# Sixteen expert units of the way in split beside pass A's front and read back; three slots beside each ranking unit

## The chip, the cores and the metric

The kernel runs on one core of a Trainium2 chip. The metric is the device time of one execution in microseconds. The kernel before was timed three times: 3121.53, 3127.26 and 3132.98 us, so its median is 3127.26 us. The profile is of a separate execution.

Engine names are those of the profile: PE is TensorE (PEld its weight loads), DVE is VectorE, ACT is ScalarE, POOL is GpSimd and SP is SyncE, which here only issues transfers.

## The reference, cut to what matters

The reference is one encoder layer on 1024 tokens of width 1024:

```python
h   = LN(x) * (1 + scale1) + shift1            # scale, shift, gate from silu(c) @ w_cond
u, v, gB, gC, z, ga, gb = split(h @ w_in)      # "the front"
yA  = gelu(u) * (W_s @ LN(gelu(v)) + b)        # spatial gating inside 128-position blocks
yB  = gB * conv3_causal(gC * z)
m   = sigmoid(ga) * (yA @ P_A) + sigmoid(gb) * (yB @ P_B)
x   = LN(alpha * x + gate1 * (m @ W_o))
h2  = LN(x) * (1 + scale2) + shift2
# experts: 8 heads, product keys, top 16 of 16384 experts per head and token
q       = h2 @ w_q
s1, s2  = q_half0 @ keys0.T, q_half1 @ keys1.T
top 16 of s1[i] + s2[j]  ->  idx, gate = softmax(top)
act     = gelu(sum_d expert_u[idx] * h2)       # "the way in"
ffn     = sum_k gate * act * expert_v[idx]     # "the way out"
x   = LN(alpha * x + gate2 * ffn)
```

All of it is float32 in the reference.

## The kernel before

**Two passes over the tokens.** Pass A is token blocks 0 to 2 (384 tokens), pass B blocks 3 to 7 (640 tokens). Both go through the front: units of 1 MB of weights, named V (4), C (12), U (4), M (16), O (4), and Q (8, one for each head's query). For pass B the experts are computed densely: 64 units E of `expert_u` (the way in, 256 experts a unit), then 64 units W of `expert_v` (the way out) in 32 groups of two. For pass A the chosen rows are gathered: 384 slots (3 blocks x 8 heads x 16), and for each slot one gathered row of `expert_u` (a dot product with h2 on DVE, `u_row`, L1050) and one of `expert_v` (a weighted sum on DVE, `v_row`, L1059). POOL issues these gathers, each 128 rows of 4 KB. The table `SECTION` says how many slots are worked off beside which unit of pass B.

**Split weights.** Every product is done with float16 halves: a 1 MB float32 unit is multiplied by 256 and split into a high and a low half, and each output takes three matmuls (high x high, high x low, low x high; L1626 to L1628). The split of unit n takes a load into one of two `stage` buffers (SP, L555), the high half by ACT (`make_hi`, L712, `w<-stage`) and the low half by DVE (`make_lo`, L954), both into slot n mod 4 of `w`. The split of unit n+4 is done after unit n has been evacuated. In pass A the 48 front units are split and both halves are also stored to `hl_dram` (1 MB, SP, L535); pass B reads them back from there straight into `w` (L564), without ACT and DVE.

**The order.** `_order` writes the units out in one list, `UNITS`, and every engine goes through this list: PE in `feature_unit` and `token_tile`, ACT and DVE in a loop over the list, SP in `load`. `CONVERTED` says which units are split, `V_OF` numbers them. SP issues in order. `load` of split number v first stores the halves of number v-2 to `hl_dram` and waits for `lo_done` of number v-2, which is what makes its stage buffer free. Beside the loads of pass A's front SP also issues `cond_pair`, 1 MB of `w_cond` after every second unit, 16 times; DVE takes their dot products (L1032).

**The ranking.** Beside the units E0 to E35 DVE also ranks pass B's scores (`rank`, in pieces, 8 heads). Then DVE makes the softmax (`gates`, L1359 to L1363, at E37), PE transposes indices and gates (L1794, after E38), and DVE copies them (`idx_t`, L1388, at E39). Beside E40 to E59 one-hot products spread the gates ("spreading units"). Before the change a unit E0 to E39 has 2 or 3 slots in turn, E40 to E59 have 2, E60 to E63 have 4, and the 30 first groups of the way out share the rest, 5 or 6 each. The rows land in rings of buffers: 6 buffers ("rank") for E0 to E36, 4 ("own") for E37 to E39.

Of the kernel before, what the change touches and what calls it, by code (L numbers as in the profile page):

```python
# [10 lines left out]
F16 = mybir.dt.float16  # L11
# [40 lines left out]


def _order():

    order = [("A", kind, u) for kind in "VCUMO" for u in range(COUNT[kind])]
    order += [("B", "V", u) for u in range(4)]
# [20 lines left out]
N_OF = {u: n for n, u in enumerate(UNITS)}  # L78
CONVERTED = [x == "A" or kind in "EW" for x, kind, _ in UNITS]
V_OF = [sum(CONVERTED[:n]) for n in range(len(UNITS))]  # L80
N_FRONT_CONV = sum(COUNT.values())


def _tiles():

    at, first, number = 0, [], []
    for x, kind, u in UNITS:
        if kind == "W":
            k = 0
        elif kind in "VO":  # L90
            k = NBLK[x]
        else:
            k = 2 if x == "A" else 4
        first.append(at)
        number.append(k)
        at += k
    return first, number
# [32 lines left out]
def _stores():  # L130

    seen, at = [0] * NW, {}
    for n in range(len(UNITS)):
        if CONVERTED[n] and V_OF[n] < N_FRONT_CONV:
            seen[n % NW] += 1
            at[n] = seen[n % NW]
    return at


STORES = _stores()  # L140
CONV_N = [n for n in range(len(UNITS)) if CONVERTED[n]]


# [47 lines left out]
def _sections():  # L191
# [6 lines left out]
    for e in range(2 * NGRP):  # L198
        k["B", "E", e] = 2 + e % 2 if e < E_SPREAD else 2 if e < E_SPREAD + N_SPREAD else 4
    groups = NGRP - 2  # L200
# [77 lines left out]
def trunk_layer(nc, x, c_row, w_cond, b_col, w_front, ln_g, ln_b, w_spat, b_spat, conv_w,  # L278
                ln1_g, ln1_b, keys_t, u_units, v_units, u_rows, v_rows, ln2_g, ln2_b, out):
    with ExitStack() as ctx:  # L280
# [150 lines left out]

        hl_dram = nc.dram_tensor("hl_dram", [48, P, 2, 2048], F16).ap()
        mod_dram = nc.dram_tensor("mod_dram", [48, P], F32).ap()
# [97 lines left out]
        def _(sp):  # L531
            def store_hl(n):
                sp.wait_ge(lo_done, V_OF[n] + 1)
                f = FRONT[UNITS[n][1]] + UNITS[n][2]
                sp.dma_start(hl_dram[f], w[:, n % NW]).then_inc(hl_stored[n % NW], 16)  # L535

            stored = [0]

            def store_to(v):

                while stored[0] <= min(v, N_FRONT_CONV - 1):
                    store_hl(CONV_N[stored[0]])
                    stored[0] += 1

            def load(n):
                x, kind, u = UNITS[n]
                if CONVERTED[n]:
                    v = V_OF[n]
                    store_to(v - 2)
                    if v >= 2:  # L550
                        sp.wait_ge(lo_done, v - 1)
                    if (x, kind, u) in (("B", "E", 0), ("B", "E", 1)):
                        sp.wait_ge(row_used, FRONT_ROWS)
                    src = u_units[u] if kind == "E" else v_units[u] if kind == "W" else w_front[FRONT[kind] + u]
                    sp.dma_start(stage[:, v % 2, :], src).then_inc(stage_in[v % 2], 16)  # L555
                    return
                f = FRONT[kind] + u
                m = N_OF["A", kind, u]
                if CONVERTED[n - NW]:
# [24 lines left out]
            sp.dma_start(ws_t, w_spat).then_inc(ws_in, 16)  # L584
            n_a = len([u for u in UNITS if u[0] == "A" and u[1] != "Q"])
            for n in range(4, n_a):
                load(n)
                if 4 <= n < 36 and n % 2 == 0:
                    cond_pair(8 + (n - 4) // 2)
                if n == 5:  # L590
# [119 lines left out]
        def _(act):  # L710
# [89 lines left out]
            for n, (x, kind, u) in enumerate(UNITS):  # L800
                if kind == "W":
                    break
                t = T_OF[n]
                if (x, kind, u) in H_AT:
# [133 lines left out]
        def _(dve):  # L938
# [497 lines left out]
            for n, unit in enumerate(UNITS):  # L1436
                x, kind, u = unit
                if kind == "W":
                    break
                if x == "A" and kind != "Q" and n % 2 == 0 and n >= 2 and pair < n_pairs:  # L1440
                    cond_dots(pair)
# [174 lines left out]
        def _(pe):  # L1616
# [105 lines left out]
            for n, (x, kind, u) in enumerate(UNITS):  # L1722
                if kind == "W":
                    break
                hl = (h_hi[x], h_lo[x])
                if (x, kind, u) == ("A", "M", 13):
# [155 lines left out]
```

## Time and profile before

| | |
|---|---|
| median of three runs | 3127.26 us |
| profiled execution, its own time | 3120.44 us |
| its span, first to last instruction | 3118.6 us |
| PE busy | 2916.0 us (94%) |
| DVE busy | 2555.4 us (82%) |
| ACT busy | 840.0 us (27%) |
| POOL busy | 1026.4 us (33%) |
| bytes moved by DMA | 917.52 MB, mean 294 GB/s |

Busy shares are averages over stages with different limits, so they are read stage by stage. Pass A's front is about 40 to 410 us, pass B's front to about 1110 us, E0 to E39 to about 1770 us, the spreading units and E60 to E63 to about 2240 us, and the way out from there to the end. A matmul's duration in a row is longer than its distance to the next one, since matmuls overlap in the pipeline: how fast PE goes is read from how many matmuls it starts in a stretch. PEclk 1.00 is 2.4 GHz, 0.50 is 1.2 GHz. Times of DMA are from issue to landing.

### The profile page before, as it was taken

The page shows a single profiled execution, that of the slowest core. Times are in us where ns is not written, and L with a number is a line of the kernel's source. Part 1 is how long each engine was busy: PE and PEld are TensorE (multiplying, and loading weights), DVE is VectorE, ACT ScalarE, POOL GpSimd, SP SyncE. Part 2 cuts the span into 40 slices and gives each one's busy share as a digit, 9 for nine tenths or more (in the row PEclk, how much of TensorE's full clock was granted, in tenths as well). Part 3 has the DMA queues.
Part 4 walks back from the last instruction along what each step waited for, and adds up shares of the span by engine and source line. Part 5 has one row for each costly group of instructions (what it writes and reads, how often), then busy time and mean ns, then how long its engine had stood idle before and what let it go on. Part 6 is the DMA issues. An engine that isn't in the chain of part 4 may idle for free.

```text
span 3118.6 us, 47106 instructions
## 1 busy us (share of the span) xinstructions
PE 2916.0 (94%) x19088; PEld 1914.8 (61%) x19088; DVE 2555.4 (82%) x4744; ACT 840.0 (27%) x1242; POOL 1026.4 (33%) x778
## 2 busy tenths in 40 slices
PE   4899999997998799999999699999789999999997
PEld 3565686765776566677777488888534444444443
DVE  5865556998777678999999788888589999999878
ACT  3333432211111332222223133333222222222220
POOL 0000000004665024444454422222455555555410
PEclk8999999998999899999999899999899999999999
DMA  8888653435999257788888788888999999999972
GB/s 344 306 312 315 238 193 122 136 129 193 344 395 351 88 201 286 298 302 312 307 323 304 291 288 283 289 291 292 354 371 396 398 395 394 398 390 408 349 265 116
DMA packets 266233, 917.52 MB, mean 294 GB/s; under 512 B 20464, under 2 KB 102432, under 8 KB 222752
## 3 DMA queue, kind: packets, MB, share of 16 engines
q1 hardware_dynamic: 63968, 427.91, 35.8%
q0 software_dynamic: 110592, 402.70, 34.6%
q10 hardware_dynamic: 91456, 83.89, 8.3%
q8 instruction: 151, 2.47, 0.3%
q14 instruction: 66, 0.54, 0.0%
HBM read 771.79 MB, written 142.63 MB: 293 GB/s over the span
## 4 chain that ended last, share of the span: by engine, by line
PE 39%; DVE 7%; DMA 3%; issue 2%; POOL 1%; ACT 0%; DVEq 0%; POOLq 0%
PE psU L1626 7%; PE psU L1627 7%; PE psU L1628 7%; PE psX L1627 5%; PE psX L1628 5%; PE psX L1626 5%; PE psX L1778 5%; DMA rows<-in_v_rows,idx_sp 3%; DVE acc_sp L1059 1%; DVE w L954 1%; POOL rows L705 1%; DMA Z<-in_v_rows,idx_sp 0%; DVE rows L1050 0%; DVE Z L1278 0%; DVE Z L1268 0%
## 5 line engine op out<-in xcount | busy, mean ns | idle before, releaser
L1626 PE MATMUL psU<-hB,w 128*128 128x320 f16 (+1 forms) x3072 | 923.7, 301 | 13.3 <-DVE hB L1025 6.9
L1628 PE MATMUL psU<-hB,w 128*128 128x320 f16 (+1 forms) x3072 | 920.5, 300 | 0.0
L1627 PE MATMUL psU<-hB,w 128*128 128x320 f16 (+1 forms) x3072 | 920.4, 300 | 0.0
L712 ACT ACTIVATE w<-stage 128x2048 f16<-128x2048 f32 x176 | 335.9, 1910 | 540.7 <-PE psX L1628 368.6
L954 DVE SCALAR_TENSOR_TENSOR w<-stage,w 128x2048 f16<-128x2048 f32 x176 | 402.4, 2287 | 93.0 <-ACT w L712 92.9
L705 POOL DMA_INDIRECT rows<-in_u_rows,idx_sp x217 | 286.4, 1320 | 525.1 <-DVE rows L1050 364.7
L1626 PEld LDWEIGHTS psU<-hB,w 128*128 128x128 f16 x3072 | 304.5, 99 | 128.0 <-DVE hB L1025 7.6
L1628 PEld LDWEIGHTS psU<-hB,w 128*128 128x128 f16 x3072 | 301.3, 98 | 119.6 <-issue 0.8
L1627 PEld LDWEIGHTS psU<-hB,w 128*128 128x128 f16 x3072 | 304.6, 99 | 112.8 <-issue 0.8
L705 POOL DMA_INDIRECT rows<-in_v_rows,idx_sp x219 | 288.2, 1316 | 245.7 <-DVE rows L1050 142.2
L1626 PE MATMUL psU<-w,Z 128*128 128x512 f16 (+1 forms) x768 | 268.8, 350 | 52.7 <-DVE Z L1428 30.3
L1059 DVE SCALAR_TENSOR_TENSOR acc_sp<-rows,weight_sp,acc_sp 128x1024 f32<-128x1024 f32 x219 | 275.8, 1288 | 47.2 <-DMA rows<-in_v_rows,idx_sp 34.5
L1626 PE MATMUL psX<-w,Z 128*128 128x512 f16 x768 | 291.1, 379 | 3.1 <-DVE Z L1549 3.1
L1627 PE MATMUL psX<-w,Z 128*128 128x512 f16 x768 | 291.1, 379 | 0.0
L1628 PE MATMUL psX<-w,Z 128*128 128x512 f16 x768 | 291.1, 379 | 0.0
L1050 DVE SCALAR_TENSOR_TENSOR rows<-rows,h_sp 128x1024 f32<-128x1024 f32 x217 | 259.3, 1222 | 26.6 <-DMA rows<-in_u_rows,idx_sp 25.3
L1627 PE MATMUL psU<-w,Z 128*128 128x512 f16 (+1 forms) x768 | 268.4, 349 | 0.0
L1628 PE MATMUL psU<-w,Z 128*128 128x512 f16 (+1 forms) x768 | 268.1, 349 | 0.0
L712 ACT ACTIVATE Z<-psU 128x320 f32<-128x320 f32 (+3 forms) x224 | 99.9, 453 | 518.5 <-PE psU L1628 496.0
L712 ACT ACTIVATE R<-psU 128x320 f32<-128x320 f32 (+1 forms) x296 | 123.9, 427 | 393.7 <-PE psU L1628 393.4
L1627 PE MATMUL psU<-Z,w 128*128 128x384 f16 (+1 forms) x640 | 206.1, 322 | 0.0
L1628 PE MATMUL psU<-Z,w 128*128 128x384 f16 (+1 forms) x640 | 206.0, 322 | 0.0
(252 smaller groups left out, 4504.4 us busy)
## 6 DMA issues: line engine op xcount, KB each, us to landing
stage<-in_u_units SPq DMA_DIRECT2D x64, 1024.0 KB, 8.9
stage<-in_v_units SPq DMA_DIRECT2D x64, 1024.0 KB, 7.8
stage<-in_w_front SPq DMA_DIRECT2D x48, 1024.0 KB, 7.6
hl_dram<-w SPq DMA_DIRECT2D x48, 1024.0 KB, 5.6
w<-hl_dram SPq DMA_DIRECT2D x48, 1024.0 KB, 7.8
a_dram<-R ACTq DMA_DIRECT2D x64, 640.0 KB, 8.3
g_dram<-Z ACTq DMA_DIRECT2D x20, 2048.0 KB, 15.3
Z<-a_dram SPq DMA_DIRECT2D x32, 1280.0 KB, 11.7
```

What stands on the lines that cost most here:

```text
L705: pool.indirect_dma_start(row_at[r], None, u_rows if table == "u" else v_rows, bass.IndirectOffsetOnAxis(ap=idx_sp[:, slot:slot + 1], axis ...
L712: return nc.scalar.activation(dst, src, func, scale=scale)
L954: V.scalar_tensor_tensor(w[:, n % NW, 1, :], stage[:, v % 2, :], WS, w[:, n % NW, 0, :], ALU.mult, ALU.subtract).then_inc(lo_done, 1)
L1050: V.scalar_tensor_tensor(row_at[r], row_at[r], 1.0, h2_sp[:, slot % SB, :], ALU.mult, ALU.mult, accum_out=dots[:, c % 8, j:j + 1]).then_in ...
L1059: V.scalar_tensor_tensor(dst, row_at[r], weight_sp[:, slot:slot + 1], dst, ALU.mult, ALU.add).then_inc(row_used, 1)
L1626: mm(ps, lhs[0](k), rhs[0](k), start=start and s == 0, stop=False)
L1627: mm(ps, lhs[0](k), rhs[1](k), start=False, stop=False)
L1628: last = mm(ps, lhs[1](k), rhs[0](k), start=False, stop=stop and s == n - 1)
L1778: ins = mm(ps[:, t * P:(t + 1) * P], oh_keys[:, q % 4, 0, :, t], oh_gate[:, q % 4, c, :, t], start=(c == 0), stop=(c == 1))
```

## The change

1. `EARLY` names the expert units E1, E3, ..., E31 (16 units). Each gets a new entry ("P", "P", u) in the unit list of pass A's front: after the 9th unit of pass A, the 11th, and so on to the 39th (after C4, C6, ..., O2). A P entry is loaded into `stage`, split by ACT and DVE into its slot of `w` and stored to `hl_dram`, but PE has no work for it.
2. In pass B these 16 units are no longer split; they are read from `hl_dram` into `w`, as the front's units are. `hl_dram` grows from 48 to 64 units. `home` says where the halves of a unit lie.
3. `SECTION`: units E0 to E35 have 3 slots each, E36 to E39 have 2. The way out's groups get 4 or 5 instead of 5 or 6. The sum over E0 to E63 goes from 156 to 172 slots of 384.
4. `cond_pair` and the dots of w_cond keep their places by counting pass A's own units, without P.

```diff
+EARLY = list(range(1, 33, 2))
 def _order():
-    order = [("A", kind, u) for kind in "VCUMO" for u in range(COUNT[kind])]
+    order = []
+    for kind in "VCUMO":
+        for u in range(COUNT[kind]):
+            order.append(("A", kind, u))
+            at = sum(x == "A" for x, _, _ in order)
+            if at > 8 and at % 2 == 1 and (at - 9) // 2 < len(EARLY):
+                order.append(("P", "P", EARLY[(at - 9) // 2]))
...
-CONVERTED = [x == "A" or kind in "EW" for x, kind, _ in UNITS]
+CONVERTED = [x in "AP" or kind == "W" or kind == "E" and u not in EARLY for x, kind, u in UNITS]
...
+def home(n):
+    x, kind, u = UNITS[n]
+    if kind in "PE":
+        return sum(COUNT.values()) + EARLY.index(u), N_OF["P", "P", u]
+    return FRONT[kind] + u, N_OF["A", kind, u]
...
-        k["B", "E", e] = 2 + e % 2 if e < E_SPREAD else 2 if e < E_SPREAD + N_SPREAD else 4
+        k["B", "E", e] = 3 if e < E_SPREAD - 4 else 2 if e < E_SPREAD + N_SPREAD else 4
...
-        hl_dram = nc.dram_tensor("hl_dram", [48, P, 2, 2048], F16).ap()
+        hl_dram = nc.dram_tensor("hl_dram", [N_STORED, P, 2, 2048], F16).ap()
...
                 if kind == "W":
                     break
+                if x == "P":
+                    make_hi(n + NW)
+                    continue
...
+                if x == "P":
+                    make_lo(n + NW)
+                    continue
```

**SP, pass A's front.** In the list of the kernel before, about the tenth load of a unit, a pair of units has two loads, two stores and one load of w_cond:

```order
L535 DMA hl_dram<-w 128x4096
L555 DMA stage<-in_w_front 128x2048
L535 DMA hl_dram<-w 128x4096
L555 DMA stage<-in_w_front 128x2048
L568 DMA hB<-in_w_cond 128x2x1024
```

The same place in the changed kernel (L552 is the store, L572 the load into `stage`, L584 `cond_pair`):

```order
L552 DMA hl_dram<-w 128x4096
L572 DMA stage<-in_u_units 128x2048
L552 DMA hl_dram<-w 128x4096
L572 DMA stage<-in_w_front 128x2048
L552 DMA hl_dram<-w 128x4096
L572 DMA stage<-in_w_front 128x2048
L584 DMA hB<-in_w_cond 128x2x1024
```

One load of `u_units` and one store have come in for each pair of units; everything else stands as it did.

**DVE, the last ranking units.** Before, from the split beside E37 (the first row) to the copies of the transposed indices at E39 (L1388):

```order
L954 SCALAR_TENSOR_TENSOR w<-stage,w 128x2048
L1359 TENSOR_REDUCE Z<-Z 128x40
L1361 RECIPROCAL Z<-Z 128x40
L1363 TENSOR_TENSOR Z<-Z 128x640
L1050 SCALAR_TENSOR_TENSOR rows,dots<-rows,h_sp 128x1024 x3
L1059 SCALAR_TENSOR_TENSOR acc_sp<-rows,weight_sp,acc_sp 128x1024 x3
L1072 SCALAR_TENSOR_TENSOR weight_sp<-dots,gate_sp 128x2
L954 SCALAR_TENSOR_TENSOR w<-stage,w 128x2048
L1050 SCALAR_TENSOR_TENSOR rows,dots<-rows,h_sp 128x1024 x2
L1059 SCALAR_TENSOR_TENSOR acc_sp<-rows,weight_sp,acc_sp 128x1024 x2
L1072 SCALAR_TENSOR_TENSOR weight_sp<-dots,gate_sp 128x3
L1388 CAST Z<-psX 128x384
```

And in the changed kernel (L975 is the split, L1071 and L1080 the rows, L1409 the copy):

```order
L975 SCALAR_TENSOR_TENSOR w<-stage,w 128x2048
L1380 TENSOR_REDUCE Z<-Z 128x40
L1382 RECIPROCAL Z<-Z 128x40
L1384 TENSOR_TENSOR Z<-Z 128x640
L1071 SCALAR_TENSOR_TENSOR rows,dots<-rows,h_sp 128x1024 x2
L1080 SCALAR_TENSOR_TENSOR acc_sp<-rows,weight_sp,acc_sp 128x1024 x2
L1093 SCALAR_TENSOR_TENSOR weight_sp<-dots,gate_sp 128x3
L975 SCALAR_TENSOR_TENSOR w<-stage,w 128x2048
L1071 SCALAR_TENSOR_TENSOR rows,dots<-rows,h_sp 128x1024 x2
L1080 SCALAR_TENSOR_TENSOR acc_sp<-rows,weight_sp,acc_sp 128x1024 x2
L1093 SCALAR_TENSOR_TENSOR weight_sp<-dots,gate_sp 128x3
L1409 CAST Z<-psX 128x384
```

Here one slot fewer stands beside E37. Further up, beside E0 to E35, every even unit has one slot more, and 16 of the splits are gone.

## Rows read from the trace of the kernel before

**Rows 1.** Busy us by stretch: PE, PEld, DVE, ACT, POOL; then PEclk, DMA share, GB/s
```profile
100.00:340.00 240.00, 234.26 (x1434) 142.63 (x1432) 161.05 (x180) 82.86 (x90) 0.00 (x0) 0.99 0.84 317
...
1125.00:1760.00 635.00, 600.77 (x4417) 436.19 (x4416) 585.11 (x1663) 163.89 (x286) 303.07 (x224) 0.98 0.82 303
...
2280.00:3000.00 720.00, 720.00 (x3338) 326.39 (x3337) 659.57 (x705) 174.27 (x110) 384.84 (x275) 1.00 0.98 385
```

**Rows 2.** DMA issues of the page: KB each, median us to landing
```profile
stage<-in_w_front SPq DMA_DIRECT2D x48, 1024.0 KB, 7.6
hl_dram<-w SPq DMA_DIRECT2D x48, 1024.0 KB, 5.6
...
Z<-in_w_cond SPq DMA_DIRECT2D x12, 1024.0 KB, 10.3
```

**Rows 3.** ACT in order of time: evacuations that end units, 7.8 us apart
```profile
246.30 0.49 ACT L712 ACTIVATE Z<-psU 128x384 f32<-128x384 f32 x1 [3.35 <-PE psU L1628]
...
254.10 0.49 ACT L712 ACTIVATE Z<-psU 128x384 f32<-128x384 f32 x1 [3.35 <-PE psU L1628]
...
261.90 0.49 ACT L712 ACTIVATE Z<-psU 128x384 f32<-128x384 f32 x1 [3.35 <-PE psU L1628]
```

**Rows 4.** The costliest groups of the page: the two halves of a split
```profile
L712 ACT ACTIVATE w<-stage 128x2048 f16<-128x2048 f32 x176 | 335.9, 1910 | 540.7 <-PE psX L1628 368.6
L954 DVE SCALAR_TENSOR_TENSOR w<-stage,w 128x2048 f16<-128x2048 f32 x176 | 402.4, 2287 | 93.0 <-ACT w L712 92.9
```

**Rows 5.** SP in order of time: load number 9, the first that moves
```profile
112.50 0.33 SPq L535 DMA_DIRECT2D hl_dram<-w  x1
112.87 0.44 SPq L555 DMA_DIRECT2D stage<-in_w_front  x1
```

**Rows 6.** SP in order of time: the last load of pass A's front
```profile
359.48 0.33 SPq L535 DMA_DIRECT2D hl_dram<-w  x1
359.85 2.24 SPq L555 DMA_DIRECT2D stage<-in_w_front  x1
```

**Rows 7.** DVE in order of time: the last low half of pass A's front
```profile
376.60 2.28 DVE L954 SCALAR_TENSOR_TENSOR w<-stage,w 128x2048 f16<-128x2048 f32 x1
```

**Rows 8.** ACT in order of time: last evacuations of O2 and of O3
```profile
402.10 0.38 ACT L712 ACTIVATE acc_sp<-psU 128x256 f32<-128x256 f32 x1 [2.24 <-PE psU L1628]
...
409.96 0.38 ACT L712 ACTIVATE acc_sp<-psU 128x256 f32<-128x256 f32 x1 [2.24 <-PE psU L1628]
```

**Rows 9.** Short stretches of pass A's front, columns as in rows 1
```profile
120.00:140.00 20.00, 20.00 (x125) 12.05 (x124) 14.14 (x15) 8.34 (x9) 0.00 (x0) 1.00 0.99 389
...
232.00:236.00 4.00, 1.44 (x9) 0.67 (x7) 1.93 (x3) 2.29 (x2) 0.00 (x0) 1.00 0.99 303
236.00:240.00 4.00, 3.35 (x11) 1.61 (x12) 4.00 (x5) 0.00 (x0) 0.00 (x0) 0.58 1.00 417
```

**Rows 10.** Waits of PE, 1700 to 1770 us: total, times, longest
```profile
PE psX L1794 <- DVE Z L1388: 22.1, 1, 22.1
PE psX L1794 <- DVE Z L1363: 5.7, 1, 5.7
```

**Rows 11.** DVE groups, 1125 to 1760 us: busy us, mean ns, idle before
```profile
L1059 DVE SCALAR_TENSOR_TENSOR acc_sp<-rows,weight_sp,acc_sp 128x1024 f32<-128x1024 f32 x76 | 96.1, 1289 | 27.4 <-DMA rows<-in_v_rows,idx_sp 18.5 <-issue 8.5
L1050 DVE SCALAR_TENSOR_TENSOR rows<-rows,h_sp 128x1024 f32<-128x1024 f32 x80 | 95.0, 1222 | 12.4 <-DMA rows<-in_u_rows,idx_sp 11.4
L954 DVE SCALAR_TENSOR_TENSOR w<-stage,w 128x2048 f16<-128x2048 f32 x40 | 91.6, 2290 | 0.0
```

**Rows 12.** Waits of DVE, 1700 to 1770 us
```profile
DVE acc_sp L1059 <- DMA rows<-in_v_rows,idx_sp: 10.4, 5, 4.2
DVE acc_sp L1059 <- issue: 4.5, 1, 4.5
```

More of the change, by code:

```diff
@@ L78 @@
 N_OF = {u: n for n, u in enumerate(UNITS)}
-CONVERTED = [x == "A" or kind in "EW" for x, kind, _ in UNITS]
+CONVERTED = [x in "AP" or kind == "W" or kind == "E" and u not in EARLY for x, kind, u in UNITS]
 V_OF = [sum(CONVERTED[:n]) for n in range(len(UNITS))]
-N_FRONT_CONV = sum(COUNT.values())
+N_STORED = sum(COUNT.values()) + len(EARLY)
 def _tiles():
@@ L87, in _tiles @@
     for x, kind, u in UNITS:
-        if kind == "W":
+        if kind in "WP":
             k = 0
@@ L133, in _stores @@
     for n in range(len(UNITS)):
-        if CONVERTED[n] and V_OF[n] < N_FRONT_CONV:
+        if CONVERTED[n] and V_OF[n] < N_STORED:
             seen[n % NW] += 1
@@ L533, in store_hl @@
                 sp.wait_ge(lo_done, V_OF[n] + 1)
-                f = FRONT[UNITS[n][1]] + UNITS[n][2]
-                sp.dma_start(hl_dram[f], w[:, n % NW]).then_inc(hl_stored[n % NW], 16)
+                sp.dma_start(hl_dram[home(n)[0]], w[:, n % NW]).then_inc(hl_stored[n % NW], 16)
             stored = [0]
             def store_to(v):
-                while stored[0] <= min(v, N_FRONT_CONV - 1):
+                while stored[0] <= min(v, N_STORED - 1):
                     store_hl(CONV_N[stored[0]])
@@ L551, in load @@
                         sp.wait_ge(lo_done, v - 1)
-                    if (x, kind, u) in (("B", "E", 0), ("B", "E", 1)):
+                    if v in (N_STORED, N_STORED + 1):
                         sp.wait_ge(row_used, FRONT_ROWS)
-                    src = u_units[u] if kind == "E" else v_units[u] if kind == "W" else w_front[FRONT[kind] + u]
+                    src = u_units[u] if kind in "PE" else v_units[u] if kind == "W" else w_front[FRONT[kind] + u]
                     sp.dma_start(stage[:, v % 2, :], src).then_inc(stage_in[v % 2], 16)
                     return
-                f = FRONT[kind] + u
-                m = N_OF["A", kind, u]
+                f, m = home(n)
                 if CONVERTED[n - NW]:
@@ L584, in _ @@
             sp.dma_start(ws_t, w_spat).then_inc(ws_in, 16)
-            n_a = len([u for u in UNITS if u[0] == "A" and u[1] != "Q"])
+            n_a = N_OF["B", "V", 0]
+            pairs = 8
             for n in range(4, n_a):
                 load(n)
-                if 4 <= n < 36 and n % 2 == 0:
-                    cond_pair(8 + (n - 4) // 2)
+                if UNITS[n][0] == "A" and n >= 4 and pairs < 24 and sum(u[0] == "A" for u in UNITS[:n]) % 2 == 0:
+                    cond_pair(pairs)
+                    pairs += 1
                 if n == 5:
@@ L1439, in _ @@
                     break
-                if x == "A" and kind != "Q" and n % 2 == 0 and n >= 2 and pair < n_pairs:
+                if x == "P":
+                    make_lo(n + NW)
+                    continue
+                if x == "A" and kind != "Q" and n >= 2 and pair < n_pairs and sum(v[0] == "A" for v in UNITS[:n]) % 2 == 0:
                     cond_dots(pair)
@@ L1724, in _ @@
                     break
+                if x == "P":
+                    continue
                 hl = (h_hi[x], h_lo[x])
```

## The prediction

> **What bounds the kernel now.** I read the busy shares by stretch first, then the waits of PE, then each engine in order of time where PE waits. In pass A's front PE is busy 234 of 240 us while the DMA engines are busy 84% of the time at 317 GB/s [rows 1]: PE sets the pace, and the transfers are not far behind. A unit takes 7.8 us there [rows 3]. In the stage of the ranking units PE is busy 601 of 635 us, but DVE 585 of 635 [rows 1], and at its end PE stands still for 22.1 + 5.7 us until DVE has made the gates and copied the transposed indices [rows 10]. DVE is the engine that is late there, and its own waits are for gathered rows [rows 11, 12]: the length of this stage is DVE's work. On the way out PE is busy 720 of 720 us at full clock, and it starts 3338 matmuls of 512 columns in 720 us, one in 215.7 ns, against 512 / 2.4 GHz = 213.3 ns [rows 1]. DVE is at 92% and DMA at 98% there without holding PE up.
>
> **Way out: gain 0.** The change takes 16 slots from the way out, 16 x (1.289 + 1.222) = 40 us of DVE [rows 11] and 16 MB of gathers. PE is at 99% of its rate and waits for neither engine. The most that could come is 720 x (215.7 - 213.3) / 215.7 = 8 us; I take 0.
>
> **Pass A's front: transfers.** Per pair of units the kernel before moves two loads, two stores and one pair of w_cond, each 1 MB [rows 2]: 5 x 1.049 = 5.24 MB in 15.6 us, 336 GB/s. The change adds a load and a store for each pair: 7.34 MB in the same 15.6 us would be 470 GB/s. What the engines can do: 317 GB/s at a share of 0.84 is 377 GB/s at a full share [rows 1], and the best 20 us of this front show 389 [rows 9]. So 7.34 MB take 7.34 / 0.377 = 19.5 us: the transfers become the bound, by 3.9 us a pair.
>
> The DMA page of the Trainium skill ("DMA: Bandwidth & Descriptors", Specifications) puts the limit of the memory at about 358 GB/s per core. Rows 9 show 389 in 20 us, so here the trace does not agree; by the page a period would take 20.5 us, and the sum below would be 13 us larger.
>
> **Pass A's front: the stage ring.** There are two stage buffers. One of them goes round like this: issue 0.4 us, landing 7.6 us [rows 2], high half 1.91, low half 2.29 [rows 4], and about 0.2 us of semaphores: 12.4 us for a load, so 6.2 us a load with two buffers, 18.6 us for three loads. This is nearly the same as 19.5, so where w_cond is moved too the transfers decide (19.5), and where it is not (6.29 MB, 16.7 us) the ring decides (18.6).
>
> **Pass A's front: the sum.** The first P entry is load number 9, which before was issued at 112.9 us [rows 5]; pass A's last unit O3 was number 39, issued at 359.9 [rows 6], and becomes number 55. From 9 to 55 there are 46 loads: 13 periods of three with w_cond, 13 x 19.5 = 253.5 us, and 7 loads of 6.2 = 43.4. O3 is issued at 112.9 + 297 = 410 us, 50 us later. Before, its low half was ready at 376.6 + 2.3 = 378.9 [rows 7], and PE began it when O2 was through, at 402.1 [rows 8]: a lead of 23 us, which is used up first. After: 410 + 0.4 + 7.6 + 1.9 + 2.3 = 422 us against 402, +20 us. To this comes that the ring does not run ideally: ACT makes the high half only after it has evacuated a unit, and DVE makes the low half after the convolution, merge and w_cond work that stands before it in its order. With two limits so close together (18.6 and 19.5) such delays add up instead of hiding. I take 1 us for each of about 14 periods, somewhat less than one product of w_cond with c (1.2 us, like the row of the same size in rows 11): +14. **Front: +34 us.** From both sides: if nothing but bytes counts, 16 x 2.10 = 33.6 MB / 0.377 = 89 us of transfers, less the free share of 100 to 340 us, 0.16 x 240 = 38, less the lead of 23, and less what the easier last 7 loads leave (some 10): +18. If every load lands only after 10.3 us, as w_cond does [rows 2], the ring takes 15.1 / 2 = 7.6 us a load: 46 x 7.6 = 348 us, O3's load at 461, so +71. ACT and DVE themselves have room: 83 and 161 of 240 us busy [rows 1], and 1.9 and 2.3 more per pair of 15.6 us. After the front pass B's units run on PE alone, so the delay is not made good later.
>
> **Ranking units.** DVE's list up to the copies at E39 has 97 slots beside E0 to E38 before and 114 after, 17 more: 17 x 2.51 = 42.7 us. It loses 16 low halves: 16 x 2.29 = 36.6 [rows 11]. Net +6; since instructions overlap a little in the trace, +5. The 16 units read back cost the same 1 MB as before, SP issues them when PE has left the slot (unit n-4), and PE needs them three units later, some 39 us: hidden. ACT loses 16 high halves; nobody waits for them. Row waits: in this stage DVE is idle 27.4 + 12.4 us before rows in `rows` [rows 11], some 0.4 us a slot. 17 more slots, with 17 MB more on DMA engines that are busy 82% [rows 1], make +7; the units E37 and E38, whose rows share four buffers and behind which 10.4 + 4.5 us are waited [rows 12], have one slot fewer: -4. **Ranking: +8 us.** Bounds: -10, if the 15 us of rows 12 go altogether, and +25, if the row waits grow by half. The wait of PE at the gates stays and grows by this amount.
>
> **Sum.** 34 + 8 = +42 us: 3120.4 + 42 = 3162 us for an execution like the profiled one. That one is 7 us under the median of the three runs, so I put the median after at 3127.3 + 42 = **3169 us**.
>
> **Rivals.**
> 1. *The front hides it, and the ranking stage gets shorter (faster).* The lead of 23 us and the free 16% of the DMA engines swallow the 33.6 MB, and with two slots each beside E36 to E39 the row waits before the copies go (-10). Median 3117. Point of decision: 46 loads would have to pass in 247 + 23 = 270 us, 5.9 us each, so a period in 17.6 us, which is 417 GB/s. The rows of this front show that only for 4 us [rows 9]. Chance 0.07; and 0.06 that the front costs so little that the two cancel (3118 to 3137).
> 2. *The ring is slower than computed.* Landing goes to 10 us, since each load stands behind a store and a pair of w_cond in the queue: 22 us a period, +37 over the forecast: 3206. For it: loads of w_cond land in 10.3 us [rows 2]. Against it: the loads before landed in 7.6 at 84% busy engines. Chance 0.15.
> 3. *PE's clock falls.* Every period PE would starve for some 4 us. After 2.6 us without work from 232 to 236 us the granted clock of the next stretch is 0.58, close to 1.2 GHz [rows 9]. If half of the matmuls of each period run at 1.2 GHz, a pair of units takes 15.6 x 1.5 = 23.4 us, over the 19.5 of the transfers: +3.9 x 14 = 55 over the forecast, 3224. Against it: a slow stretch of 4 us costs 2 us of PE's work, and a period has 3.9 us to spare. Chance 0.06. The page "TensorE: Matmul & The Clock Gate" of the Trainium skill (HAM oscillation) tells of such a kernel, which waits for a transfer in each round and starts each round at the slow clock; rows 9 agree as to the fall, and no row of before shows it repeated.
> 4. *The ranking stage pays more than the front.* The rows come late with three slots beside each unit and six buffers: ranking +25 and front as forecast: 3186. It lies in the range; chance 0.06.
>
> **How the numbers follow.** The forecast has 0.60, with its own range of 3145 to 3195 (front +18 to +55, ranking 0 to +15). The range 3135 to 3206 leaves out rival 1, most of rival 3 and a part of rival 2, some 0.2. A change under 0.3%, about 9 us, could not be told from none for this kernel. Faster is rival 1, 0.07; same is 0.06; slower is the rest, 0.87.
>
> **What the changed profile would show.** DMA share at 0.95 or more at 370 to 390 GB/s from about 115 to 400 us; PE waiting for the low half of `w` in each period, with granted clock below 1.00 in some of them; load number 55 issued at about 410 to 425 us; the end of O3 near 440 us instead of 410. The stage from E0 to the copies of the indices 0 to 15 us longer, with PE's wait at the transposes of about 35 us. The way out as long as before, with DVE's busy share lower by 40 us. It would be wrong if PE stayed busy through the front (rival 1), if periods took 22 us or more (rival 2), or if the way out became shorter by more than 8 us.

## The result: slower by 3.4%, outside the forecast range

| | median us | runs |
|---|---|---|
| before | 3130.12 | 3121.53 to 3134.93 (4) |
| after | 3236.66 | 3229.83 to 3243.77 (4) |

The ratio is 1.0344, with an interval of 1.0311 to 1.0377. That is +106.5 us where +42 was forecast, and 3236.7 against a range that ended at 3206. The profiled execution of after took 3243.8 us with a span of 3242.0, 123.4 us above the span of before. It lies 7 us over the median of its runs and the one of before lay 10 us under its own, so 17 of the 123 belong to the two executions and not to the change.

The span divides at the last evacuation of O3 (end of pass A's front), the first store of a ranking unit (E0), the copies of the transposed indices, and the first unit of the way out:

| stage | before | after | difference | forecast |
|---|---|---|---|---|
| start to the end of O3 | 410.0 | 478.6 | +68.6 | +34 |
| to E0 | 721.7 | 742.0 | +20.3 | 0 |
| E0 to the copies of the indices | 625.5 | 664.8 | +39.3 | +8 |
| to the way out | 520.4 | 515.5 | -4.9 | 0 |
| way out | 841.0 | 841.1 | +0.1 | 0 |

The forecast had the two right places and was low at both by about the same amount.

**Pass A's front.** Busy us of PE, PEld, DVE, ACT and POOL, then granted clock, DMA share and GB/s, first in the whole front of before, then of after with four short stretches of it:

```profile
100.00:410.00 310.00, 297.52 (x1910) 191.03 (x1909) 191.77 (x225) 113.75 (x144) 0.00 (x0) 0.98 0.78 288
```

```profile
100.00:479.00 379.00, 307.74 (x1898) 194.66 (x1897) 226.70 (x237) 139.33 (x159) 0.00 (x0) 0.90 0.86 323
200.00:220.00 20.00, 5.22 (x33) 5.03 (x33) 14.42 (x15) 6.49 (x5) 0.00 (x0) 0.65 0.93 349
220.00:240.00 20.00, 20.00 (x117) 11.86 (x116) 11.82 (x13) 6.74 (x7) 0.00 (x0) 0.92 0.45 168
380.00:400.00 20.00, 6.35 (x35) 4.15 (x32) 13.23 (x15) 7.36 (x7) 0.00 (x0) 0.67 0.97 379
400.00:420.00 20.00, 12.97 (x74) 8.24 (x75) 7.79 (x9) 9.78 (x14) 0.00 (x0) 0.73 0.63 244
```

PE does the same work, idles 71.3 us instead of 12.5, and its busy time grows by 10.2 because the granted clock falls from 0.98 to 0.90. The DMA share is not the 0.95 at 370 to 390 GB/s that the forecast named but 0.86 at 323: PE and the transfers stand still in turn. From 200 to 220 us PE works 5 of 20 us while DMA runs at 0.93, and in the next 20 us PE works throughout while DMA falls to 0.45. So neither of the two is the bound on its own.

Who waits for whom, in after's front: waits of PE (total, times, longest), then of ACT and DVE.

```profile
PE psU L1650 <- DVE w L975: 21.4, 6, 5.4
PE psX L1707 <- DVE h_sp L1198: 14.8, 1, 14.8
PE psX L1755 <- DVE modc L1470: 12.6, 1, 12.6
PE psU L1650 <- issue: 10.7, 1, 10.7
PE psX L1696 <- DVE Z L1475: 8.1, 1, 8.1
```

```profile
ACT w L730 <- DMA stage<-in_w_front: 102.1, 30, 5.2
ACT w L730 <- DMA stage<-in_u_units: 66.2, 12, 7.2
```

```profile
DVE w L975 <- ACT w L730: 109.8, 39, 6.2
DVE acc_sp L1240 <- DMA Z<-in_ln_b: 15.6, 1, 15.6
```

Only 21 us of PE's waits are for a low half, as forecast. Most of the others are for DVE work that has nothing to do with a split (h_sp of the mixing, modc, Z): it stands on DVE behind a split that waits for ACT, which waits for a load. The 10.7 us to which the profile gives no releaser ("issue") are of the same kind: PE's matmul at 263.81 us reads the `acc_sp` that DVE writes from 262.75 to 263.71 (L1214), behind the split of 258.96. In its whole front (100 to 410 us) ACT of the kernel before waited for stage loads 8 times, 17.1 us in all; here it is 42 times and 168.3 us. One such place, ACT, DVE and PE at the mixing in order of time (the bracket holds the idle time ahead and its releaser):

```profile
205.13 1.91 ACT L730 ACTIVATE w<-stage 128x2048 f16<-128x2048 f32 x1 [2.96 <-DMA stage<-in_w_front]
...
212.00 1.91 ACT L730 ACTIVATE w<-stage 128x2048 f16<-128x2048 f32 x1 [4.20 <-DMA stage<-in_w_front]
```

```profile
213.94 2.29 DVE L975 SCALAR_TENSOR_TENSOR w<-stage,w 128x2048 f16<-128x2048 f32 x1 [2.12 <-ACT w L730]
216.15 2.48 DVE L1198 TENSOR_TENSOR h_sp<-psX,Z 128x512 f32<-128x512 f32 x4
```

```profile
216.88 1.44 PE L1707 MATMUL psX<-Z,acc_sp 128*128 128x128 f32 x5 [14.78 <-DVE h_sp L1198]
```

DVE's h_sp at 216.15 follows the split of 213.94 in its list without a gap, that split had to wait for ACT, and ACT for the load. PE stands for 14.8 us; for the same wait before it stood 2.4 us.

The last load of this front on SP, in after (compare [rows 6], 359.85):

```profile
444.23 0.43 SPq L572 DMA_DIRECT2D stage<-in_w_front  x1
...
453.92 0.43 SPq L619 DMA_DIRECT2D Z<-in_ln_b  x1
```

46 loads pass in 444.2 - 111.0 = 333.2 us, 7.24 us each, where the forecast had 297 + 14.

**The ranking stage.** E0 to the copies of the indices of before, and the same of after:

```profile
1131.00:1757.00 626.00, 592.56 (x4361) 429.67 (x4359) 576.18 (x1621) 162.41 (x283) 297.36 (x219) 0.98 0.82 304
```

```profile
1220.00:1885.00 665.00, 603.92 (x4359) 432.40 (x4357) 583.81 (x1633) 130.60 (x269) 314.21 (x253) 0.96 0.83 310
```

DVE's work grew by 7.6 us (forecast: 5 to 6), its idle time by 31. Waits of DVE there, in before and in after (the 10.4 and 4.5 of [rows 12] are part of the first):

```profile
DVE acc_sp L1059 <- DMA rows<-in_v_rows,idx_sp: 18.5, 13, 4.2
DVE rows L1050 <- DMA rows<-in_u_rows,idx_sp: 11.4, 7, 3.2
DVE acc_sp L1059 <- issue: 8.5, 6, 4.5
```

```profile
DVE rows L1071 <- DMA rows<-in_u_rows,idx_sp: 30.1, 11, 7.0
DVE acc_sp L1080 <- DMA rows<-in_v_rows,idx_sp: 28.2, 14, 6.8
DVE acc_sp L1080 <- issue: 11.8, 7, 6.3
```

PE's wait at the copies of the end is 18.1 + 1.8 us instead of 22.1 + 5.7 [rows 10]. But PE now waits long for evacuations, which cost it 6.4 us in before (1.3 for R, 5.1 for Z):

```profile
PE psU L1650 <- ACT R L730: 39.7, 9, 9.1
```

ACT is not busy (130.6 of 665 us). It stands in its own list at the activation of the dots. This is ACT, then PE, about 1450 us, and the stretch just before (columns as in rows 1):

```profile
1449.63 0.20 ACT L730 ACTIVATE dots<-dots 128x3 f32<-128x3 f32 x1 [16.30 <-DVE rows L1071]
1449.74 1.40 ACT L730 ACTIVATE R<-psU 128x320 f32<-128x320 f32 x4
```

```profile
1450.31 0.43 PE L1650 MATMUL psU<-hB,w 128*128 128x320 f16 x1 [6.21 <-ACT R L730]
```

```profile
1433.00:1449.60 16.60, 11.10 (x82) 7.76 (x80) 16.40 (x93) 0.33 (x1) 2.65 (x3) 0.96 0.65 254
```

Four evacuations for PE stand behind a wait of 16.3 us for DVE's dots. DVE does not wait for a row there: it is busy 16.40 of 16.60 us, mostly with a piece of the ranking that stands ahead of the dots in its list. It is so at each of the four waits of PE for ACT over 2 us between 1340 and 1720 us (4.7, 6.2, 7.9 and 3.5 us): DVE is already behind, by its own work and by the rows it waited for earlier, and PE feels it where a piece of ranking comes on top. At 1327.68, where DVE did wait 6.96 us for a u row, PE stood for 0.91 us only. In after this wait of ACT for dots comes to 325.7 us in 36 places, in before to 40.6 + 4.2 in 12.

### The profile page after: what moved, and what is told of

Same layout as the page of the kernel before. It is cut to its first block, busy times and chain, and to the rows that moved or that the text cites. A ratio compares the mean times of both kernels' runs of the same rounds, so it can differ in the third digit from the quotient of the medians.

```text
span 3242.0 us, 47170 instructions
## 1 busy us (share of the span) xinstructions
PE 2951.6 (91%) x19088; PEld 1923.7 (59%) x19088; DVE 2560.8 (79%) x4744; ACT 832.9 (26%) x1242; POOL 976.0 (30%) x778
## 4 chain that ended last, share of the span: by engine, by line
PE 38%; DVE 7%; DMA 4%; issue 2%; POOL 1%; ACT 0%; DVEq 0%; POOLq 0%
PE psU L1650 6%; PE psU L1651 6%; PE psU L1652 6%; PE psX L1651 5%; PE psX L1650 5%; PE psX L1652 5%; PE psX L1804 5%; DMA rows<-in_v_rows,idx_sp 3%; DVE acc_sp L1080 1%; DVE w L975 1%; POOL rows L723 1%; POOL Z L723 0%; DMA Z<-in_v_rows,idx_sp 0%; DVE Z L1071 0%; DVE Z L1299 0%
## 5 line engine op out<-in xcount | busy, mean ns | idle before, releaser
L1650 PE MATMUL psU<-hB,w 128*128 128x320 f16 (+1 forms) x3072 | 931.7, 304 | 53.4 <-ACT R L730 39.7
L975 DVE SCALAR_TENSOR_TENSOR w<-stage,w 128x2048 f16<-128x2048 f32 x176 | 402.6, 2289 | 177.3 <-ACT w L730 171.1
L723 POOL DMA_INDIRECT rows<-in_v_rows,idx_sp x268 | 327.0, 1220 | 272.8 <-DVE rows L1071 127.5
L1080 DVE SCALAR_TENSOR_TENSOR acc_sp<-rows,weight_sp,acc_sp 128x1024 f32<-128x1024 f32 x268 | 337.0, 1290 | 53.1 <-DMA rows<-in_v_rows,idx_sp 36.4
L723 POOL DMA_INDIRECT rows<-in_u_rows,idx_sp x178 | 221.9, 1247 | 450.1 <-DVE rows L1071 305.7
L1071 DVE SCALAR_TENSOR_TENSOR rows<-rows,h_sp 128x1024 f32<-128x1024 f32 x178 | 214.2, 1221 | 43.4 <-DMA rows<-in_u_rows,idx_sp 43.0
L1650 PE MATMUL psU<-Z,w 128*128 128x384 f16 (+1 forms) x640 | 209.3, 327 | 18.3 <-DVE w L975 18.3
L1651 PE MATMUL psU<-Z,w 128*128 128x384 f16 (+1 forms) x640 | 208.9, 326 | 0.0
L1652 PE MATMUL psU<-Z,w 128*128 128x384 f16 (+1 forms) x640 | 208.6, 326 | 0.0
```

The costliest lines, as they stand in the source:

```text
L723: pool.indirect_dma_start(row_at[r], None, u_rows if table == "u" else v_rows, bass.IndirectOffsetOnAxis(ap=idx_sp[:, slot:slot + 1], axis ...
L975: V.scalar_tensor_tensor(w[:, n % NW, 1, :], stage[:, v % 2, :], WS, w[:, n % NW, 0, :], ALU.mult, ALU.subtract).then_inc(lo_done, 1)
L1071: V.scalar_tensor_tensor(row_at[r], row_at[r], 1.0, h2_sp[:, slot % SB, :], ALU.mult, ALU.mult, accum_out=dots[:, c % 8, j:j + 1]).then_in ...
L1080: V.scalar_tensor_tensor(dst, row_at[r], weight_sp[:, slot:slot + 1], dst, ALU.mult, ALU.add).then_inc(row_used, 1)
L1650: mm(ps, lhs[0](k), rhs[0](k), start=start and s == 0, stop=False)
L1651: mm(ps, lhs[0](k), rhs[1](k), start=False, stop=False)
```

## The experiments

All are timed beside the kernel before on the same chip, and a ratio is to that one. "Front" is the end of O3 against before's 410.0; "stage" is E0 to the copies of the indices, before 625.5. Both come from the one profiled execution of each. How far they can be trusted: four kernels have the front of after unchanged (after, e2, e7, e8), and its excess over before is 68.6 to 74.2 us in them; five have the stage of after unchanged (after, e3, e5, e6, e9), and it is 662.0 to 666.4 us long in them.

**Each half alone.** e1 is before with the new slots only; e2 is after with the old slots.

```diff
 e1 (in before)
-        k["B", "E", e] = 2 + e % 2 if e < E_SPREAD else 2 if e < E_SPREAD + N_SPREAD else 4
+        k["B", "E", e] = 3 if e < E_SPREAD - 4 else 2 if e < E_SPREAD + N_SPREAD else 4
 e2 (in after): the same line the other way
```

> The kernel before with the new SECTION alone: 3 slots beside E0 to E35, 2 beside E36 to E39, no early units, all 64 units split in pass B. Theory A (the ranking stage's length is DVE's work, and rows come late only where a split no longer stands between two sections of six rows): 17 slots more x 2.4 us = +40 us in the stage, row waits of DVE there about as before (30 to 45 us), way out unchanged: 3165 to 3175 us, and PE's stalls sit in the stage and at the gates. Theory B (three slots beside each unit alone make the six row buffers too few): row waits 60 us and more, 3195 us or more. Front of pass A as before in both.

> The changed kernel with the old SECTION (2 and 3 slots in turn), so the sixteen early units alone. Theory A (front and ranking stage add up separately): the end of O3 again near 478 us (+68), the stretch from there to E0 again up to 20 us longer, and the ranking stage shorter, since DVE has 35 us less and PE's wait of 28 us at the gates goes: -28, so 3127 + 60 to 90 - 28 = 3165 to 3190 us. Theory B (reading the units back delays rows or evacuations in the ranking stage by itself): ranking stage no shorter than before, 3195 to 3215 us.

Measured: e1 3174.80, ratio 1.0138 (1.0094 to 1.0182), front -1.7, stage +58.7. e2 3183.43, ratio 1.0166 (1.0122 to 1.0210), front +74.2, stage -16.7. Both times lie in the range of their theory A (3165 to 3175, 3165 to 3190), though the waits for rows of e1 (58.1 us, below) are nearer to the 60 of theory B than to the 30 to 45 of theory A. The medians add: 44.3 + 52.9 = 97 of 106.5. So the front is the work of the early splits, and the longer stage that of the slots: 58.7 - 16.7 = +42, against +39.3 in after. Each half is slower than before, though by less than 2%. In the stage of e1, PE and DVE wait as in after:

```profile
PE psU L1626 <- ACT R L712: 50.1, 11, 9.1
```

```profile
DVE acc_sp L1059 <- DMA rows<-in_v_rows,idx_sp: 28.8, 11, 5.2
DVE rows L1050 <- DMA rows<-in_u_rows,idx_sp: 16.2, 9, 6.3
DVE acc_sp L1059 <- issue: 13.1, 7, 3.7
```

**The mixing ahead of the split.** In e3 DVE's mix_out of pass A stands ahead of the low half, not behind it.

```diff
+                if unit == ("A", "C", 11):
+                    dve.wait_ge(bs_in, 16)
+                    mix_out(x)
 ...                make_lo(n + NW)
```

> The changed kernel, but at the unit C11 of pass A DVE evacuates the spatial mixing (mix_out) before it makes the low half of unit n+4, for whose load it waits. Theory A (a large part of the front's loss is that DVE's and ACT's in-order lists make PE's own chain wait for a load that is four units ahead): PE's wait of 14.8 us before the mixing goes, the long load gap behind it shrinks, and the end of O3 comes 10 to 20 us earlier: 3218 to 3228 us. Theory B (the bytes alone set the front's length, 16 x 2 MB more at about 377 GB/s): the end of O3 stays within 3 us, since the transfers take as long: 3237 us.

Measured: 3222.75, ratio 1.0309 (1.0261 to 1.0357), front +64.1. PE's wait there is 12.1 us instead of 14.8. The end of O3 comes 4.5 us earlier, where theory A had 10 to 20 and theory B under 3; that is no more than fronts of the same code differ by (5.6 us). The median is 14 us lower and so in the range of theory A, but the intervals overlap, and in the profiles 17 of the 22 us between the two lie in pass B's front, which this edit does not touch. So a gain is not shown. The wait itself stays, because mix_out needs C11's evacuation, and that stands on ACT behind a high half which waits for its load. Mending one place of a chain over three lists did not remove the wait.

**Half as many.** e4 takes every fourth expert unit (E1, E5, ..., E29) and one place in four, so 8 P entries, with the old slots.

```diff
-EARLY = list(range(1, 33, 2))
+EARLY = list(range(1, 33, 4))
-            if at > 8 and at % 2 == 1 and (at - 9) // 2 < len(EARLY):
-                order.append(("P", "P", EARLY[(at - 9) // 2]))
+            if at > 8 and at % 4 == 1 and (at - 9) // 4 < len(EARLY):
+                order.append(("P", "P", EARLY[(at - 9) // 4]))
```

> Eight early units (E1, E5, ..., E29) instead of sixteen, one after every fourth unit of pass A, old SECTION. Per four units 12.6 MB in 31.2 us of PE's work = 403 GB/s wanted against 377: 33.4 us. Theory B (bytes): front +18 less the lead of 23 us, so 0 to +5; ranking stage -18 (8 splits of 2.2 us): 3110 to 3118 us. Theory A (in-order lists): the front loses 10 to 25 us, as each P still makes DVE and ACT wait for a load: 3120 to 3135 us.

Measured: 3140.31, ratio 1.0028 (1.0008 to 1.0047), front +26.6, stage -7.7. An entry costs 26.6 / 8 = 3.3 us of front here and 74.2 / 16 = 4.6 in e2: the price rises with the density. It gives back about 1 us each in the ranking stage (16.7 / 16, 7.7 / 8), so neither sixteen nor eight pay at these places. The time is over both theories' ranges (at most 3135), and the front a little over the 10 to 25 of theory A. Fewer than eight were not tried.

**What in a P entry costs.** These leave out parts of the P entries' work and keep their places in all lists: e5 stores only 256 of the 2048 columns of each half; e6 also loads only 256 columns; e9 also splits only 256. The units' halves are then incomplete, so `home` is changed too: the sixteen early units of pass B read the halves of sixteen front units instead, 1 MB each as before.

```diff
 e5
+                if UNITS[n][0] == "P":
+                    sp.dma_start(hl_dram[home(n)[0]][:, :, 0:256], w[:, n % NW, :, 0:256]).then_inc(hl_stored[n % NW], 16)
+                    return
 e6
+                    if x == "P":
+                        sp.dma_start(stage[:, v % 2, 0:256], src[:, 0:256]).then_inc(stage_in[v % 2], 16)
+                        return
 e9 (make_hi and make_lo)
+                m = 256 if UNITS[n][0] == "P" else 2048
```

> The changed kernel, but a P entry stores only 512 bytes of each half and partition row instead of 4 KB (the early units of pass B read other units' halves of the same size instead, so their products are not the experts'). Loads, splits and all orders stay. A period of the front then moves 6.29 MB, not 7.34. Theory B (bytes decide): 16.7 us a period or the ring's 18.6, instead of the 21 measured: the end of pass A's front comes 30 to 38 us earlier than in the changed kernel. Theory A (the in-order lists of ACT and DVE decide): at most 15 us earlier. Ranking stage as in the changed kernel: in all 3200 to 3207 (B) or 3222 and more (A).

> As the kernel with the short store of the P entries, and their load too brings only 1 KB per partition instead of 8 KB. ACT and DVE still make all sixteen early splits. Theory B (transfers): the front is as long as before the change within 5 us, so the whole is about 3127 + 40 (ranking stage) = 3167 us. Theory A: the added 1.9 us on ACT, 2.3 us on DVE and the waits in their lists still cost, front +15 to +30: 3182 to 3197 us.

> As the kernel with short loads and stores of the P entries, and ACT and DVE also split only 256 of their 2048 columns. What is left of a P entry is its place: one of four slots of w, one of two stage buffers in turn, one position in every engine's list. That kernel's front was 31 us longer than before. Theory E (engine time of the splits, 16 x 4.2 us, standing in the lists): the front's excess falls to under 12 us, 3170 to 3178 us. Theory F (the place: loads and splits look four positions ahead, of which only two or three are units with work for PE): the excess stays at 20 to 31 us, 3185 to 3196 us.

| | median | ratio | front | next load into a P entry's stage buffer, us (mean of 15) |
|---|---|---|---|---|
| after | 3236.66 | 1.0344 (1.0311 to 1.0377) | +68.6 | 16.7 |
| e5 store small | 3219.45 | 1.0254 (1.0224 to 1.0285) | +51.1 | 16.0 |
| e6 and load small | 3195.82 | 1.0183 (1.0158 to 1.0208) | +31.5 | 14.3 |
| e9 and split small | 3189.19 | 1.0180 (1.0153 to 1.0207) | +27.1 | 11.9 |

Taken away in this order, the bytes of the stores make 17.5 of the 68.6 us, those of the loads 19.6, the engines' time for the splits 4.4 (which is within the spread of one profile), and 27.1 stay when an entry moves and computes next to nothing. The 17.5 lie between the two theories of e5 (at most 15; 30 to 38), the 31.5 left in e6 just over theory A's 15 to 30. With hardly any bytes or work left, an entry still holds one of the two stage buffers, and one of the four slots of `w`, for which PE has nothing to do. ACT of e9 in front of the mixing shows it:

```profile
170.54 0.42 ACT L736 ACTIVATE w<-stage 128x256 f16<-128x256 f32 x1 [3.08 <-DMA stage<-in_u_units]
179.59 1.91 ACT L736 ACTIVATE w<-stage 128x2048 f16<-128x2048 f32 x1 [8.64 <-DMA stage<-in_w_front]
```

The small load was issued at 165.79 and is used at 170.54. SP issued the next real load at 172.08, when the other buffer was free, and ACT stood for it 8.64 us. The forecast's 12.4 us for a full load twice and 11.9 once give (12.4 + 12.4 + 11.9) / 2 = 18.4 us for three loads, over the 15.6 that PE needs for a pair of units: 2.8 x 15 = 42 us late, less some of the lead of 23 us. As an estimate, that is 19 to 42 us, and 27 lies in it. Theory E wanted an excess under 12 us, theory F, the place of the entry, 20 to 31 and 3185 to 3196 us: F holds. Whether the stage buffer or the slot of `w` holds more of it was not separated.

**The rows' buffers.** e7 takes one of the six buffers of rows away in the ranking stage:

```diff
+    "rank": [0, 1, 2, 3, 8]
```

> The changed kernel with five instead of six buffers for the gathered rows beside E0 to E36. Theory C (rows come late because a section of six rows uses every buffer, and each is free again only when DVE has read it): DVE's waits for rows in the ranking stage rise from 73 us by 40 to 100 us, and the time with them: 3275 to 3330 us. Theory D (rows come late because the DMA engines are full): within 10 us of the changed kernel, 3237 us. Front of pass A unchanged in both.

Measured: 3267.11, ratio 1.0421 (1.0395 to 1.0447), front +70.4, stage 698.5, +33.7 over after. Waits of DVE and PE in its stage:

```profile
DVE rows L1071 <- DMA rows<-in_u_rows,idx_sp: 42.6, 15, 7.6
DVE acc_sp L1080 <- DMA rows<-in_v_rows,idx_sp: 28.8, 30, 6.0
DVE acc_sp L1080 <- issue: 19.9, 9, 6.1
```

```profile
PE psU L1650 <- ACT R L730: 63.5, 15, 10.8
```

With one buffer fewer DVE waits 104.7 us for rows and issue instead of 72.5, and the stage is longer by about as much; PE waits longer for evacuations. So the number of buffers is a limit of this stage; whether a seventh would help was not tried. The direction is that of theory C; the time of 3267 is below the 3275 to 3330 that it gave, and the added wait of 32 us below its 40 to 100.

**Contention.** e8 reads back only 256 of 2048 columns of the 16 early units, so that 14 of the 16 MB read back in this stage are not moved (their halves are incomplete).

```diff
+                if kind == "E":
+                    sp.dma_start(w[:, n % NW, :, 0:256], hl_dram[f][:, :, 0:256]).then_inc(w_in[n % NW], 16)
+                    return
```

> The changed kernel, but the sixteen early units are read back in pass B with only 512 bytes of each half and partition row instead of 4 KB; the rest of w keeps what stood there, so these products are not the experts'. 15 MB fewer in the ranking stage. Theory D (rows come late because the DMA engines are crowded): DVE's row waits in the stage fall from 73 us to 40 to 55, the whole is 20 to 30 us shorter: 3207 to 3217 us. Theory C (rows come late because six rows use all six buffers and the pause between two sections is short): row waits stay within 10 us, 3227 to 3237 us.

Measured: 3231.19, ratio 1.0317 (1.0288 to 1.0347), stage 653.4, 11.4 under after. The waits for rows by DMA fall from 60.7 to 12.3 + 23.1 + 2.1 = 37.5 us (those for issue rise from 11.8 to 24.2), PE's for ACT from 39.7 to 31.1. By the medians it is 5 us, within the intervals, and 3231 lies in the range of theory C. The stage is 9 us under the shortest of the five with the stage of after, so the bytes do cost something there, as theory D had it, but they are the smaller part: without them the stage is still 28 us over before.

**Other slots, without early splits.** If three slots beside a unit are the trouble, two beside each should help. These are before with another table; the sum over all units stays 384.

```diff
 c2
+        k["B", "E", e] = 2 + (e % 4 == 3) if e < E_SPREAD else 2 + e % 2 if e < E_SPREAD + N_SPREAD else 4
 c4
+        k["B", "E", e] = 2 if e < E_SPREAD else 3 if e < E_SPREAD + N_SPREAD else 4
 c5
+        k["B", "E", e] = 2 if e < E_SPREAD else 2 + e % 2 if e < E_SPREAD + N_SPREAD else 4
```

> A version against the kernel before, from what the slots alone cost: ten slots taken from E0 to E39 (2 beside each unit, 3 beside every fourth) and put beside E40 to E59 (2 and 3 in turn). No early units. Theory (the ranking stage is DVE's work plus late rows, the spreading units and the way out are PE's): the stage loses 10 x 2.4 us of DVE and some row waits, so 20 to 28 us, which is PE's wait at the gates; the spreading units stay PE-bound (DVE 86% -> 91%): 3098 to 3110 us. Rival (the spreading units become DVE-bound or their rows late): 3120 to 3135 us.

> A version against the kernel before: 2 slots beside each unit E0 to E39 and 3 beside each of E40 to E59 (20 slots moved). Theory: the ranking stage is DVE-bound until PE's wait at the gates is gone, 20 x 2.4 = 48 us of DVE less against a wait of 28: stage -25 to -28 us; the spreading units reach DVE 96% and DMA close to full and lose 5 to 15 us: 3105 to 3120 us. Rival: the spreading units hold: 3098 to 3104 us.

> A version against the kernel before: 2 slots beside each unit E0 to E39, 2 and 3 in turn beside E40 to E59, and ten slots more on the way out (5 or 6 a group as before, more of 6). Theory: stage -25 to -28 us, spreading units as in the version with ten slots moved (+2 to +4 us), way out unchanged since PE is at its full rate with DVE at 92%: 3098 to 3106 us. Rival (the way out is at 98% DMA share and the 10 MB more make it wait): 3110 to 3125 us.

| | median | ratio | stage |
|---|---|---|---|
| c2: 2, 2, 2, 3 beside E0 to E39 | 3108.22 | 0.9924 (0.9896 to 0.9953) | 606.2 |
| c4: 2 beside each; 3 beside E40 to E59 | 3096.10 | 0.9882 (0.9860 to 0.9905) | 596.7 |
| c5: 2 beside each; rest also on the way out | 3102.10 | 0.9887 (0.9864 to 0.9910) | 596.7 |

c4 beats both kernels, the kernel before by 1.2%: clear of the interval, though under 2%. Its time is below the 3105 to 3120 of its theory and the 3098 to 3104 of its rival; c2 and c5 lie in their ranges (3098 to 3110, 3098 to 3106). The stage of c4, and its waits of DVE for rows (another 3.2 us is for u rows in Z) and of PE at the copies:

```profile
1152.00:1749.00 597.00, 588.89 (x4359) 428.15 (x4357) 527.97 (x1558) 164.45 (x283) 247.48 (x180) 1.00 0.79 281
```

```profile
DVE acc_sp L1059 <- DMA rows<-in_v_rows,idx_sp: 4.6, 3, 2.9
...
DVE acc_sp L1059 <- issue: 2.3, 1, 2.3
```

```profile
PE psX L1794 <- DVE Z L1388: 8.8, 1, 8.8
```

PE is busy 589 of 597 us at a clock of 1.00. The 40 splits are still in this stage, as in before: they never had to go away. c4 and c5 can't be told apart.

**What the stages add up to.** DVE's busy time, its waits for rows and issue, and PE's waits for evacuations by ACT, each from the stage of one profile:

| | units with 3 slots | splits | DVE busy | DVE waits for rows | PE waits for ACT | stage |
|---|---|---|---|---|---|---|
| before | 20 | 40 | 576.2 | 41.3 | 6.4 | 625.5 |
| e1 | 36 | 40 | 617.7 | 58.1 | 54.3 | +58.7 |
| e2 | 20 | 24 | 541.9 | 50.9 | 0.0 | -16.7 |
| after | 36 | 24 | 583.8 | 72.5 | 41.2 | +39.3 |
| c2 | 10 | 40 | 550.8 | 47.1 | 3.5 | -19.3 |
| c4 | 0 | 40 | 528.0 | 10.1 | 0.0 | -28.8 |

In e1 DVE's work grows by 41.5 us and its waits for rows by 16.8, together 58.3: nearly the 58.7 of the stage. In after it is 7.6 and 31.2, together 38.8 of 39.3. Where the stage got longer, its length is DVE's work plus DVE's waits for rows, and PE's waits for ACT are the same lateness seen from PE, not a further cost. The slots alone add 16.8 us of waits (e1), fewer splits alone 9.6 (e2), both 31.2.

## Why the prediction was wrong

**Pass A's front, right in mechanism, +34 against +68.6.** The first five periods took 19.8 us (loads of `u_units` at 111.0, 129.6, 149.3, 170.5, 189.3 and 209.8), where the sum had 19.5. Two terms of the sum failed: the "1 us for each of about 14 periods" for lists in order, and the 20 us from O3's load to the end of O3 that are left once the lead of 23 us "is used up first".
- Loads: 333 us against 297 + 14, 22 us more (it began 2 us earlier, so the last load is 20 late). Most of it lies in three periods: 28.2 us at the mixing and U0 (209.8 to 238.0), 23.7 behind it, 27.1 at M13 to M15 (407.2 to 434.3). There the splits stand behind work of other kinds on DVE and ACT, and PE itself starves; while PE does not finish units, no slot of `w` comes free and DMA falls to 0.45 and 0.63. The sum treated lateness as the larger of two rates plus a constant; the entries tie PE, ACT, DVE and SP into one chain.
- Tail: from O3's load to its last evacuation the sum had 430 - 410 = 20 us. Measured 34.4: landing 8.7, high half 1.9, 9.6 in which DVE waited for ln_b and did the work queued behind it, two low halves 4.5, PE 9.7. SP issues ln_b behind the last load (at 453.92), and that load stood 50 us before the end in the kernel before, 34 us in after. The sum counted the loads of units and forgot what else stands on SP behind them. 20 + 14 is the miss of 35. No run moves ln_b, so this part is read from the rows alone.

**Rival 3, the clock, partly.** Granted clock 0.90 instead of 0.98 in this front, so the low level (1.2 of 2.4 GHz) in a part of it. PE waits for 2.6 us or more at eleven places, and at nine of them the 5 us that follow are at 0.50 to 0.66. At the other two, behind 3.42 us at 170.1 and 2.68 us at 368.2, the clock stays at 1.00. One of each kind:

```profile
346.00:351.00 5.00, 4.16 (x14) 1.97 (x15) 4.12 (x5) 1.68 (x1) 0.00 (x0) 0.50 1.00 347
...
368.00:373.00 5.00, 4.83 (x30) 2.95 (x31) 1.91 (x3) 2.67 (x3) 0.00 (x0) 1.00 1.00 383
```

It is worth the 10.2 us of PE's busy time, not the 55 of the rival. The account of the Trainium skill ("TensorE: Matmul & The Clock Gate", HAM oscillation) that was named beside it, of a kernel in which each round starts slow, fits nine of these eleven starts, not each of them.

**Rival 2, the ring slower,** had the right sign: 333.2 / 46 x 3 = 21.7 us a period against its 22. But e5, e6 and e9 show that the bytes are only a part of it: a P entry still holds its stage buffer for 11.9 us with next to none, where the sum had 12.4 for a full load, and 16.7 in after. That its price of +37 over the forecast is close to the +34.6 that came is luck: only 20 of these lie in the loads.

**The limit of the memory.** The sum by 377 GB/s stood against the Trainium skill's 358 ("DMA: Bandwidth & Descriptors", Specifications). After shows 379 GB/s over 20 us again (380 to 400), so the limit was not what failed; over the whole front it is 323, under both.

**The ranking stage, wrong in its main term, +8 against +39.3.** The step that the stage's length is DVE's work and its waits for rows held, the count of DVE's work held (+7.6 against 5 to 6), and the read-back was hidden on PE (no wait of PE for it in the profile). PE's wait at the end did not grow to some 35 us as forecast but fell to 18.1 + 1.8: PE had by then waited elsewhere, for ACT. What failed is the term for the rows, +7 and -4, from "some 0.4 us a slot": it came to +31.2. The term took the waits of before as a price of each slot. The runs show three things in its place. With six buffers, a unit of three slots needs all of them for its six rows: where no unit has three, DVE waits 10.1 us (c4), where 10, 20 and 36 have, 47.1, 41.3 and 58.1 (c2, before, e1), and one buffer fewer adds 32 (e7). With 16 splits fewer the waits are 9.6 us longer (e2), as if the splits had been time in which rows could arrive. And without most of the bytes that are read back they are 10.8 shorter (e8). Whether it matters that two units with three slots stand next to each other was not tested by itself: c2 never has two in a row, and DVE waits in it no less than in before. c2 and c4 also have fewer slots in all beside E0 to E39 (90 and 80 instead of 100), so number and spread are not separated. Rival 4 (+25) was this mechanism at a chance of 0.06, and still too small.

**The way out, right.** 841.0 and 841.1 us, with 16 slots fewer; DVE is busy 725 us in it instead of 761 (forecast: 40 less).

**Pass B's front, +20.3, not of the change as far as the runs show.** The stretch from the gates of pass A to the end of M15 in pass B took 22.6 us longer than before in this profile, but 16 in e1, 10 in e2, 4 in e3, 1 in e4, 13 in e8 and about 26 in c4. c4 changes nothing ahead of E0, and after and e3 have the same work there. So this stretch differs from one profiled execution to another without a change in its code, and that is the likely reason why differences of two profiles and of medians lie up to 30 us apart (c4: -9.5 and -40). Each kernel has one profile only, and what sets it off stays open.

## What to carry to other kernels

A unit that is put into a ring ahead of time costs its place in the ring, not only its bytes: in lists worked in order, count the entries between an engine and the next piece of work it can use, and every other transfer that is issued behind them. Where several lists wait for each other, lateness spreads through all of them, so a sum of the slowest resource plus a small constant is a lower end and not a middle. And where gathered rows pass through few buffers, look at the units whose rows fill all of them: try moving one slot from each to later units, before moving other work away. Here that made the kernel 1.2% faster, and the work moved away made it 3.4% slower.

## What the runs showed of the hardware

A load of 256 columns (128 KB) issued at 165.79 us in e9 was usable only at 170.5, 4.7 us, where a full one of 1 MB takes 7.6 [rows 2]: an eighth of the bytes is not an eighth of the time. The stores of e9 say the same: a median of 4.4 us for 128 KB and 5.0 for 1 MB. And beside 16 early units, the median landing of a 1 MB store went from 5.6 to 6.7 us, with the DMA share over the front going only from 0.78 to 0.86; in e9 it is 5.0 us at 0.76.
